# A hybrid decoder step on one core: the first tiles of the output projection taken in parts inside the end of the cache attention

## What is computed

```
n = RMSNorm(h);  p = n @ W_in
h = h + W_out [ GatedDeltaNet(p) ; MLA(p) ]
h = h + W_down relu(W_up RMSNorm(h))^2
y = RMSNorm(h)
```

```
s_past = latent_scores(q_lat, q_pe, c_past, kpe_past)
p = softmax(concat([s_past, s_new]))
out_lat = p[..., :P] @ c_past + p[..., P:] @ c_new
o = einsum('bthc,chv->bthv', out_lat, w_kv_b[..., MLA_D_NOPE:])
```

## Time and profile before

| | |
|---|---|
| median of 3 runs | 1036.35 us (1035.49 to 1036.37) |
| profiled execution | 1033.08 us, span of its trace 1031.3 us |
| mean granted TensorE clock | 0.981 of full |
| TensorE (PE) busy | 981.3 us, 95% |
| VectorE (DVE) busy | 514.1 us, 50% |
| ScalarE (ACT) busy | 446.4 us, 43% |
| GpSimd (POOL) busy | 157.1 us, 15% |
| output and MLP products (L597 to L599 with XH, NH) | 4320 matmuls, some 0.29 us each with overlap |
| weight chunk, load | 1024 KB, 4.8 us from issue to landing |

### The profile page before, as it was taken

One profiled execution on the slowest core, in us unless ns is written; L12 is line 12 of the kernel. 1 busy time (PEld: TensorE's weight loads), 2 busy tenths in 40 slices (PEclk: granted clock), 3 DMA queues, 4 the chain that ended last, 5 costly groups with the idle time before them and its releaser, 6 DMA issues.

```text
span 1031.3 us, 20653 instructions
## 1 busy us (share of the span) xinstructions
PE 981.3 (95%) x8604; PEld 850.7 (82%) x8604; DVE 514.1 (50%) x977; ACT 446.4 (43%) x964; POOL 157.1 (15%) x257
## 2 busy tenths in 40 slices
PE   4999999999989999899999899999999999999997
PEld 3988899877757556566665799999999999999996
DVE  5655867565575485355454532633343234334423
ACT  5545637566646675344444423431232134113312
POOL 1020500255511201345541000000000000000000
PEclk9999969999999999899999899999999999999998
DMA  7312111220024501477672321422222222223202
GB/s 247 116 51 83 43 42 42 58 52 11 2 65 116 208 1 33 178 252 261 242 241 91 118 83 41 144 82 83 85 100 102 82 83 83 82 85 100 104 1 87
DMA packets 31655, 102.58 MB, mean 99 GB/s; under 512 B 14023, under 2 KB 14967, under 8 KB 25218
## 3 DMA queue, kind: packets, MB, share of 16 engines
q1 hardware_dynamic: 22346, 63.50, 18.9%
q0 software_dynamic: 9216, 37.75, 10.6%
HBM read 96.45 MB, written 4.22 MB: 98 GB/s over the span
## 4 chain that ended last, share of the span: by engine, by line
PE 87%; DVE 6%; ACT 3%; issue 2%; DMA 1%; SPq 0%; DVEq 0%; ACTq 0%
PE PS L597 17%; PE PS L599 17%; PE PS L598 17%; PE PS L1086 7%; PE PS L1097 3%; PE PS L1123 3%; PE PS L732 2%; PE PS L1106 1%; PE PS L805 1%; PE PS L836 1%; PE PS L888 1%; DMA RAW<-in_w_stream 1%; PE PS L987 1%; PE PS L579 1%; PE PS L706 1%
## 5 line engine op out<-in xcount | busy, mean ns | idle before, releaser
L597 PE MATMUL PS<-XH,WH 128*128 128x272 f32 (+1 forms) x928 | 271.2, 292 | 1.8 <-DVE WL L1740 1.8
L599 PE MATMUL PS<-XH,WL 128*128 128x272 f32 (+1 forms) x928 | 270.4, 291 | 0.0
L598 PE MATMUL PS<-XL,WH 128*128 128x272 f32 (+1 forms) x928 | 269.5, 290 | 0.0
L597 PEld LDWEIGHTS PS<-XH,WH 128*128 128x128 f32 x928 | 175.9, 190 | 6.8 <-issue 4.2
L598 PEld LDWEIGHTS PS<-XL,WH 128*128 128x128 f32 x928 | 176.1, 190 | 0.0
L1232 ACT ACTIVATE WH<-RAW 128x2048 fp32r<-128x2048 f32 x46 | 88.0, 1913 | 203.1 <-PE PS L599 203.0
L599 PEld LDWEIGHTS PS<-XH,WL 128*128 128x128 f32 x928 | 175.8, 189 | 0.0
L597 PE MATMUL PS<-NH,WH 128*128 128x272 f32 x512 | 149.1, 291 | 0.8 <-DVE WL L1740 0.8
L599 PE MATMUL PS<-NH,WL 128*128 128x272 f32 x512 | 147.6, 288 | 0.0
L598 PE MATMUL PS<-NL,WH 128*128 128x272 f32 x512 | 146.6, 286 | 0.0
L1740 DVE TENSOR_TENSOR WL<-RAW,WH 128x2048 fp32r<-128x2048 f32 (+1 forms) x48 | 108.1, 2252 | 65.3 <-ACT WH L1232 64.2
(11 more groups left out here) (331 smaller groups left out, 1498.3 us busy)
## 6 DMA issues: line engine op xcount, KB each, us to landing
RAW<-in_w_stream SPq DMA_DIRECT2D x47, 1024.0 KB, 4.8
XN<-in_hin SPq DMA_DIRECT2D x4, 512.0 KB, 6.5
out_y_p<-YO SPq DMA_DIRECT2D x4, 512.0 KB, 2.7
CST<-in_big SPq DMA_DIRECT2D x1, 1132.5 KB, 13.4
SS<-in_sstate SPq DMA_DIRECT2D x1, 1024.0 KB, 5.3
out_ssm_s<-SS SPq DMA_DIRECT2D x4, 256.0 KB
CN<-in_cache,IDX POOLq DMA_INDIRECT x64
WQN<-in_wq SPq DMA_DIRECT2D x3, 256.0 KB, 5.9
```

The source lines that it names most:

```text
L597: pe.matmul(PS[:, b, 0:n], wh, xh[:, k, c:c + n], start=(k == 0), stop=False)
L598: pe.matmul(PS[:, b, 0:n], wh, xl[:, k, c:c + n], start=False, stop=False)
L599: last = pe.matmul(PS[:, b, 0:n], wl, xh[:, k, c:c + n], start=False, stop=(k == DT - 1))
```

## The change

TensorE's first two output tiles are taken in parts (`out_part(j, ks)`, the k-tiles `ks` of tile j): k 0 to 2 of tile 0 behind the last value product, k 3 of tile 0 and k 0 of tile 1 behind the transposes of ACC, k 1 to 3 of tile 1 behind the samples' output products, then k 4 to 7 of both; `big_product` goes on at tile 2. `sample_outputs` is cut in two functions for that. ScalarE makes the high part of chunk 11 in block 15 (n = 15, u = 1) and XH tiles 0 to 3 at n = 16, u = 0. VectorE makes the low part of chunk 11 in four quarters (n = 15 at u = 3, 5, 6, and n = 16 at u = 0) and XL tiles 0 to 3 at n = 16, u = 5. The waits say when the buffers beneath are free.

```diff
@@ TensorE
+            def out_part(j, ks):
+
+                for k in ks:
+                    if j == 0:
+                        pe.wait_ge(sem("split"), HALF0["out"] + k + 1)
+                    wh, wl = WH[N_IN % 2][:, k, P * j:P * j + P], WL[N_IN % 2][:, k, P * j:P * j + P]
+                    for x, (c, n) in enumerate(LATE):
+                        pe.matmul(PS[:, 2 * j + x, 0:n], wh, XH[:, k, c:c + n], start=(k == 0), stop=False)
...
-            sample_outputs()
-            big_product(N_IN, (XH, XL), mixed_ready)
+            pe.wait_ge(sem("w_split"), N_IN + 1)
+            out_part(0, range(0, 3))
+            sample_transposes()
+            out_part(0, range(3, 4))
+            out_part(1, range(0, 1))
+            sample_outputs()
+            out_part(1, range(1, 4))
+            for j in range(2):
+                out_part(j, range(4, DT)).then_inc(sem("tile_done"), 1)
+            big_product(N_IN, (XH, XL), None, first=2)
@@ ScalarE, in the loop over n and u
+                    if n == 15 and u == 1:
+                        act.wait_ge(sem("ce_pv"), 13)
+                        weights_high(N_IN)
+                    elif n == 16 and u == 0:
+                        act.wait_ge(sem("ct_used"), 3 * 15 + 1)
+                        mixed_high(range(0, 3))
+                        act.wait_ge(sem("ct_used"), 3 * 15 + 2)
+                        mixed_high(range(3, 4))
...
-            for d in range(PAIRS):
-                act.activation(XH[:, d, META:], MIXT[:, d, META:], ACT.Copy).then_inc(sem("high"), 1)
-            act.wait_ge(sem("ce_pv"), 16)
-            weights_high(N_IN)
@@ VectorE
+            def out_weights_low(i):
+
+                if i == 0:
+                    dve.wait_ge(sem("ce_pv"), 14)
+                    dve.wait_ge(sem("w_high"), N_IN + 1)
+                w, part = N_IN % 2, slice(2 * i, 2 * i + 2)
+                last = low(WL[w][:, part, :], RAW[w][:, part, :], WH[w][:, part, :])
+                if i == 3:
+                    last.then_inc(sem("w_split"), 1)
...
+                    if n == 16 and u == 0:
+                        out_weights_low(3)
...
+                    if n == 15 and u in (3, 5, 6):
+                        out_weights_low((3, 5, 6).index(u))
+                    elif n == 16 and u == 5:
+                        mixed_low(range(PAIRS))
```

More of the change, by code:

```diff
@@ L1139, in _, with sample_transposes @@
                         cache_p(n - 1)
-            def sample_outputs():
+            def sample_transposes():
                 for g in range(2):
@@ L1148, in sample_outputs @@
                 last.then_inc(sem("pe_step"), 1)
+            def sample_outputs():
                 pe.wait_ge(sem("act_step"), ACT_STEP["ol_copied"])
@@ L1155, in sample_outputs @@
                 last.then_inc(sem("pe_step"), 1)
-            def mixed_ready(j, k):
-                if j == 0:
-                    pe.wait_ge(sem("split"), HALF0["out"] + k + 1)
+            def out_part(j, ks):
[5 more added lines that the diff above has]
+                        pe.matmul(PS[:, 2 * j + x, 0:n], wh, XH[:, k, c:c + n], start=(k == 0), stop=False)
+                        pe.matmul(PS[:, 2 * j + x, 0:n], wh, XL[:, k, c:c + n], start=False, stop=False)
+                        last = pe.matmul(PS[:, 2 * j + x, 0:n], wl, XH[:, k, c:c + n], start=False, stop=(k == DT - 1))
+                return last
             def tile_reader(g):
@@ L1165, in tile_reader, with big_product @@
                 return ("a_scaled" if product % 2 else "res_added"), DT * (product // 2) + j + 1
-            tile = [22]
-            def big_product(w0, moving, ready):
-                for j in range(DT):
+            tile = [24]
+            def big_product(w0, moving, ready, first=0):
+                for j in range(first, DT):
                     w = w0 + j // 2
@@ L1653, in cache_high, with mixed_high @@
                 act.activation(CRH[:, :], PS[:, CT_BANKS[(9 * n + 8) % 4], :], ACT.Copy).then_inc(sem("ct_high"), 1)
+            def mixed_high(ds):
+                for d in ds:
+                    act.activation(XH[:, d, META:], MIXT[:, d, META:], ACT.Copy).then_inc(sem("high"), 1)
             def cache_exp(n):
@@ L1689, in _ @@
             act.wait_ge(sem("act_step"), ACT_STEP["os_copied"])
-            for d in range(PAIRS, DT):
-                act.activation(XH[:, d, META:], MIXT[:, d, META:], ACT.Copy).then_inc(sem("high"), 1)
+            mixed_high(range(PAIRS, DT))
             for w in (1, 2):
@@ L2187, in cache_copy, with mixed_low @@
                 dve.tensor_copy(CT[u][:, :], PS[:, CT_BANKS[(9 * n + u) % 4], :]).then_inc(sem("ct_dve"), 1)
+            def out_weights_low(i):
[6 more added lines that the diff above has]
+                    last.then_inc(sem("w_split"), 1)
+            def mixed_low(ds):
+                for d in ds:
+                    dve.wait_ge(sem("high"), HALF0["out"] + d + 1)
+                    low(XL[:, d, META:], MIXT[:, d, META:], XH[:, d, META:]).then_inc(sem("split"), 1)
             def cache_low(n):
@@ L2221, in _ @@
                                   ALU.mult).then_inc(sem("acc_scaled"), 1)
[L2223 to L2227, removed]
+            mixed_low(range(PAIRS, DT))
             weights_low(N_IN + 1)
```

## The result

| | before | changed |
|---|---|---|
| median of 6 runs | 1035.8 us (1033.73 to 1036.37) | 1026.89 us (1024.85 to 1028.57) |
| ratio | | 0.9915 (0.9901 to 0.9929), 8.9 us |
| profiled execution, span | 1033.08, 1031.3 us | 1028.57, 1026.7 us |
| TensorE busy, mean granted clock | 981.3 us, 0.981 | 979.0 us, 0.985 |

The two profiled executions, on the other hand, differ by only 4.6 us in span. Neither number is the worth of the change. That has to be read at the seam, and I measure it there in every profile from the start of the last value product (L1123) to the start of the residual addition of output tile 1 (VectorE, HT): **22.53 us before, 15.96 us after**, 6.57 us less.

What follows compares the result with a forecast made beforehand. TensorE was taken to bound the kernel, at 87% of the span. Waits 3.99, half-clock projection matmuls 1.6, output products 0.5 and transposes 0.4 us gave a 6.5 us gain: 1036.35 to 1029.9 us, range 1028.5 to 1033.2.

Steps and rivals of the forecast that it cites:

- TensorE's new order: From the last value product to tile 2: projection pieces fill the waits, tile 2 starting at 582.45 instead of 588.96.
- The 6.5 us of the sum: Gain up to tile 2: waits 3.99, projection matmuls at half clock 1.6, output products 0.5, transposes 0.4 us.
- ScalarE and VectorE in the attention, cost 0: Last attention blocks: moved splits fit idle gaps at 0 us; bounds 0 and 0.3 us for VectorE, 0 to 0.3 possible for ScalarE.
- Chunk 12 late next: Before tile 2: chunk 12's low part done at 580.9, wanted at 582.45, 1.5 us to spare.
- Chunk 13's load beside chunk 12: SP's queue: chunk 13 issued right behind chunk 12, which lands at 575.0 at worst, needed at 576.7; cost 0.
- the first 15 projection matmuls at half clock, 1.6: Start of the output projection: these matmuls, 575.28 to 578.77, take 1.9 us instead of 3.5, gaining 1.6.
- a rival for a clock that falls all the same after the change: At the seam: clock at half as long as before, 6.8 us; gain only 3.1 us, 1033.2 us; chance 13%.
- The step from the profiled execution to the median: Whole kernel: the runs' median, 1036.35, lay 3.3 us above the profiled 1033.08; this difference was carried over unexplained.
- The scatter that I allowed below, 0.9 us: Lower end of the range: 0.9 us for the scatter of the runs, 1035.49 to 1036.37.
- no slot too tight: Last two attention blocks and second-half XL: moved pieces push the chain; gain 5.4 us, 1031.0 us; chance 11%.
- no wait for chunk 12: At tile 2: loads side by side land chunk 12 at 579.9, 1.7 us pass the slack; 1031.6 us; chance 3%.
- nothing slower: Attention's last two blocks: moved work, 9.6 us, wholly uncovered against 6.5 gained; +3.1 us, 1039.4 us; chance 2%.

Runs made afterwards that it cites:

- e8: Changed kernel with the low part of chunk 11 in one piece instead of four quarters: 14th to 16th value product 11.79 us instead of 11.23, seam 15.96 us.
- e2: Kernel before plus 34 matmuls of no use in TensorE's three holes at the seam: 1031.36 us against 1033.43 us, ratio 0.9977.
- e10: Changed kernel with four projection matmuls before the last value product and 14 useless ones early in the cache attention: 1024.56 us, ratio 0.9917 to the kernel before.
- e12: The kernel of e10 again, beside the changed kernel on one chip: 1023.27 us, ratio 0.9918 to the kernel before.
- e5: Kernel before, unchanged, profiled a second time: seam 23.75 us, 10.2 us at half clock there.
- e6: Kernel before, unchanged, profiled a third time: seam 22.90 us, 6.8 us at half clock there.
- e7: Kernel before, unchanged, profiled a fourth time: seam 23.76 us, 10.2 us at half clock there.
- later comparisons: Changed kernel unaltered, timed twice more against the kernel before: 1025.66 us, ratio 0.9931, and 1025.16 us, ratio 0.994.
- e4: Changed kernel with its first 18 projection matmuls behind the transposes instead of the last value product: 1028.42 us, ratio 0.9945 to the kernel before.

## Why the prediction was right in its mechanism and missed in its size

*TensorE's new order: right.* Counted from the start of the last value product, I had the transposes at 4.20, the output products at 6.21, the third piece at 7.51, tile 2 at 15.82 us; the profile has 4.23, 6.27, 7.35 and 15.76. The 6.5 us of the sum are 6.57 in the two profiles. The output products took 1.08 us to the next start where I had chosen 1.3.

*ScalarE and VectorE in the attention, cost 0: right,* and e8 shows that it holds because the low part was cut in quarters; in one piece it costs 0.56 us. *Chunk 12 late next, with 1.5 us to spare: right* (1.55). *Chunk 13's load beside chunk 12: no cost,* in 568 to 576 the DMA engines moved 8 us x 265 GB/s, 2.1 MB, the two chunks, and ScalarE took chunk 12 up at 578.57.

*The term that was mis-sized* is "the first 15 projection matmuls at half clock, 1.6". It was read from one execution, in which the clock came back 3.5 us behind the first matmul. In the others it came back up to 6.1 us behind it or fell later. The seams are 0.4 to 1.2 us longer for it: 22.53 to 23.76, mean 23.24. Against e2's seam with the clock full (21.04 us) the term measured 1.5, 2.7, 1.9 and 2.7 us in the four profiles, 2.2 on average. That alone does not carry the result out of the range: with 7.3 us instead of 6.5 the forecast would have been 1029.1 us, inside it. I had a rival for a clock that falls all the same after the change, but none for a clock that was kinder in the profiled execution than in most, and so the range had too little room below.

*The step from the profiled execution to the median* failed too, and it put the result outside, together with a scatter that I took too small. I carried over 3.3 us and subtracted. The table shows where they can lie: apart from the seam itself, all scatter lies before it (406.9 to 410.0 us to the first transposes, 157.7 to 160.0 us in the attention, without e10 and e12), none behind it (442.11 to 442.20). Part of it is the clock again: e5 and e6, the two longest to the first transposes, show 6.8 us more at half clock there than the other twelve. Another part is one wait at the second scores of the attention, 2.2 us in the changed kernel's first profile, e7 and e8 and 1.2 us or less in the others. Three runs had fixed my 1036.35 us; later sets of the kernel before gave 1035.8, 1033.4, 1033.6 and 1032.1 us, the second on one chip and the last two on another; on which chip the first was run is not known, so a difference between chips is not ruled out. Of the 3.0 us by which 1029.9 missed, 0.55 are the lower median of before, 0.7 the seam. The remaining 1.7 us of the first comparison are not the seam's; later comparisons (7.1 and 6.2 us) don't show them, and which stage they came from in those runs stays open, since those were not profiled. The scatter that I allowed below, 0.9 us, was that of three runs; 22 runs of the same kernel spread over 5.8 us.

*The rivals.* No clock fall after the change in three profiles, no slot too tight (11.23 us from the 14th to the 16th value product), no wait for chunk 12, nothing slower.

## What to carry to other kernels

A hole on the bounding engine costs its own length and, as here where several stood in a row, can cost the half clock behind it (e4's single hole did not): fill it with work that is due anyway (7.3 us here), or, where there is none, with matmuls of no use (without moving anything else 2.2 us against the mean of the four seams, 1.5 us against the shortest). Move work into an engine's idle time in pieces no longer than the gaps in front of what others wait for. And take a clock term from several executions: one profile shows one of its values.

## What the runs showed that I had not expected

The time at half clock at an unchanged seam differs by 3.4 us between executions of one kernel (6.8 or 10.2 us), while the 442 us behind it, over 3300 matmuls, repeat within 0.1 us. And 14 useless matmuls at the start of the cache attention are worth about 2 us of the median: the hole they fill had brought the clock down for 6.8 us behind it in eleven of the twelve profiles without them and for 3.4 us in the twelfth, and in neither profile with them (mean clock in 410 to 425: 0.95 against 0.73).
